# Recurrent layer of a fused block: outputs and norm by tokens in column strips, state products in row strips

## The reference, cut to what matters

```python
proj = h @ w_in                                   # [512, 4 * 1024]
q_x, f_x, i_x, g_x = jnp.split(proj, [HK, 2 * HK, 2 * HK + HV], axis=-1)
f = lb + (1.0 - lb) * sigmoid(f_x);  q = heads(silu(q_x));  k = heads(1.0 - f);  v = heads(i_x)
b = cumsum(log(f)) within each chunk of 32;  b_ref = b[16], b_last = b[31] of the chunk
q_rel, k_rel = q * exp(b - b_ref), k * exp(b_ref - b)
a = where(causal, q_rel @ k_rel.T, 0.0)           # 32 x 32 in each chunk
o_intra = a @ v
q_dec, k_dec, chunk_decay = q * exp(b), k * exp(b_last - b), exp(b_last)
def step(state, xs):                              # 16 chunks in order, state 128 x 128
    o_inter = qd @ state
    state = dec[..., None] * state + kd.T @ vc
o = rms_norm(o_intra + o_inter, o_norm) * silu(g_x)   # norm over the 128 channels of the head
return o @ w_o
```

## Time and profile before

| | us |
|---|---|
| median of three runs | 2893.7 |
| lowest, highest | 2890.9, 2904.2 |
| profiled execution, span from its first to its last instruction | 2894.7 |
| PE busy | 2755.6 (95%) |
| DVE busy | 1621.2 (56%) |
| ACT busy | 1137.4 (39%) |
| POOL busy | 122.3 (4%) |

### The profile page before, as it was taken

The page is one execution under the profiler, slowest core; times in us unless marked ns, Lnnn a source line. Parts: engine busy times, 40 slices in busy tenths (PEclk is TensorE's granted clock), DMA queues, the critical chain, the costliest instruction groups (busy, mean ns, idle before and its releaser), DMA issues.

```text
span 2894.7 us, 39160 instructions
## 1 busy us (share of the span) xinstructions
PE 2755.6 (95%) x14119; PEld 2223.8 (77%) x14119; DVE 1621.2 (56%) x3030; ACT 1137.4 (39%) x1894; POOL 122.3 (4%) x106
## 2 busy tenths in 40 slices
PE   7999999999999999998998998999999989999998
PEld 5567888888888788887685886667877777788887
DVE  6335726456665662645656337765577765564461
ACT  4434322225553422223438324852355543322221
POOL 0000000000000000000130001000011110000000
PEclk9999999999999999998999989999999999999999
DMA  4112333312211233331220221013222222333232
GB/s 139 43 59 73 109 95 94 102 52 67 67 63 37 80 114 97 95 97 58 64 81 1 73 74 30 1 44 95 80 66 73 66 66 73 124 102 98 92 101 65
DMA packets 59684, 217.83 MB, mean 75 GB/s; under 512 B 6432, under 2 KB 6560, under 8 KB 59424
## 3 DMA queue, kind: packets, MB, share of 16 engines
q1 hardware_dynamic: 57920, 209.76, 23.5%
q0 software_dynamic: 1632, 6.29, 0.6%
HBM read 211.83 MB, written 4.19 MB: 75 GB/s over the span
## 4 chain that ended last, share of the span: by engine, by line
PE 81%; DVE 10%; ACT 3%; issue 3%; DVEq 2%; ACTq 0%; DMA 0%; POOL 0%; SPq 0%
PE ps L371 23%; PE ps L373 22%; PE ps L372 22%; DVE work L2095 1%; PE ps L512 1%; DVE big L3254 1%; DVEq L3312 1%; DVE work L2114 1%; DVE ring_lo L311 1%; PE ps L763 1%; PE ps L1564 1%; PE ps L1640 1%; PE ps L2020 1%; PE ps L2256 1%; ACT ring_hi L304 1%
## 5 line engine op out<-in xcount | busy, mean ns | idle before, releaser
L371 PE MATMUL ps<-a_hi,ring_hi 128*128 128x512 f32 (+1 forms) x1976 | 781.7, 396 | 42.7 <-DVE ring_lo L311 24.0
L373 PE MATMUL ps<-a_hi,ring_lo 128*128 128x512 f32 (+1 forms) x1976 | 766.4, 388 | 0.0
L372 PE MATMUL ps<-a_lo,ring_hi 128*128 128x512 f32 (+1 forms) x1912 | 739.7, 387 | 0.0
L311 DVE TENSOR_TENSOR ring_lo<-ring,ring_hi 128x1024 fp32r<-128x1024 f32 x357 | 436.7, 1225 | 519.5 <-ACT ring_hi L304 489.6
L304 ACT ACTIVATE ring_hi<-ring 128x1024 fp32r<-128x1024 f32 x377 | 396.7, 1055 | 505.8 <-PE ps L373 503.6
L371 PEld LDWEIGHTS ps<-a_hi,ring_hi 128*128 128x128 f32 x1976 | 376.5, 191 | 125.0 <-DVE ring_lo L311 18.1
L373 PEld LDWEIGHTS ps<-a_hi,ring_lo 128*128 128x128 f32 x1976 | 375.9, 190 | 76.7
L372 PEld LDWEIGHTS ps<-a_lo,ring_hi 128*128 128x128 f32 x1912 | 364.2, 190 | 70.1 <-issue 1.2
L372 PE MATMUL ps<-hid_lo,ring_hi 128*128 128x512 f32 (+1 forms) x992 | 381.0, 384 | 0.0
L371 PE MATMUL ps<-hid_hi,ring_hi 128*128 128x512 f32 (+1 forms) x928 | 354.5, 382 | 0.0
L373 PE MATMUL ps<-hid_hi,ring_lo 128*128 128x512 f32 (+1 forms) x928 | 354.2, 382 | 0.0
(11 more groups left out here) (419 smaller groups left out, 3369.3 us busy)
## 6 DMA issues: line engine op xcount, KB each, us to landing
ring<-weights SPq DMA_DIRECT2D x392, 512.0 KB, 3.6
h<-x SPq DMA_DIRECT2D x1, 2048.0 KB, 9.4
residual<-h POOLq DMA_DIRECT2D x4, 512.0 KB, 3.5
h<-residual POOLq DMA_DIRECT2D x1, 2048.0 KB, 10.9
out<-h POOLq DMA_DIRECT2D x1, 2048.0 KB, 7.9
tab<-tables SPq DMA_DIRECT2D x1, 1648.0 KB, 15.5
big<-positions SPq DMA_DIRECT2D x1, 256.0 KB, 3.4
col<-columns SPq DMA_DIRECT2D x1, 164.5 KB, 4.1
```

Of the source, the lines that this page charges most:

```text
L311: dve.tensor_tensor(lo, M.ring[:, b % RING, :], hi.bitcast(F32), ALU.subtract).then_inc(M.sem("blocks_split"), 1)
L371: pe.matmul(out, w_hi, hi, start=start, stop=False)
L372: pe.matmul(out, w_hi, lo, start=False, stop=False)
L373: return pe.matmul(out, w_lo, hi, start=False, stop=stop)
```

## The change

The state products take the turned keys as they are (`kt`, one copy of 128 partitions), and use 32 rows of the array each: keys and values of chunk r lie on partitions 32r to 32r + 31, so the matmul uses row strip r. The four strips write to four different banks (4, 5, 6, 7). All 15 that are needed come in one go before slice 5 of projection 2, behind waits on `hg_v`, `hg_keys_kept`, `hg_pairs_masked` and `hg_y`. DVE's chain waits for them once.

The outputs have tokens on the partitions: masked pairs stationary and values moving, then 32 tokens of q_dec stationary and a state moving, which uses column strip r of the array and writes partitions 32r to 32r + 31 of bank 7. The first chunk, whose state is zero, is left out. The sum over channels is then along the free axis: ACT takes four squares with an accumulator, the root at once, and after DVE's reciprocal four copies scaled by the inverse root of each token (`ot`). PE turns them back with four transposes (`turn_out`) behind projection 1 of the next head, and DVE applies gate and gain with one L1807. `total` and `spread`, L1810, the zeros of `kz` and the wait for `hg_y` before the pairs are gone.

```diff
+PAIR_BANK, KEY_BANK, OUT_T_BANK, OUT_BANK = 4, 5, 6, 7
+STATE_BANK = (PAIR_BANK, KEY_BANK, OUT_T_BANK, OUT_BANK)
...
-        self.kz = M.m[:, 0:4, :]
+        self.kt, self.ot = M.m[:, 0, :], M.m[:, 1, :]
...
-    dve.memset(R.kz, 0.0)
...
-            if k == (4 if j else 6) and between:
+            if k == 5 and between:
...
-    def states(tt, bank):
-        for r in range(4):
-            mm = pe.matmul(M.bank(bank)[:, r * P:(r + 1) * P], R.kz[:, r, tt * P:(tt + 1) * P],
-                           R.v[:, tt * P:(tt + 1) * P], start=True, stop=True)
+    def states():
+        for t in range(QT):
+            for r in range(4):
+                if 4 * t + r < N_CH - 1:
+                    rows, s = slice(CH * r, CH * r + CH), slice(t * P, (t + 1) * P)
+                    mm = pe.matmul(M.bank(STATE_BANK[r])[:, s], R.kt[rows, s], R.v[rows, s], start=True, stop=True)
         mm.then_inc(M.sem("hg_chunk_states"), 1)
-    def total(i):
-        pe.wait_ge(M.sem("hg_squared"), i + 1)
-        norm_total_pe(pe, M, M.bank(7), M.sq[:, 0, :]).then_inc(M.sem("hg_total"), 1)
-    def spread(i):
-        pe.wait_ge(M.sem("hg_inverse"), i + 1)
-        norm_spread_pe(pe, M, M.bank(7), lambda c: M.inv[:, c:c + 1].broadcast_to([P, P]))\
-            .then_inc(M.sem("hg_spread"), 1)
+    def turn_out(i):
+        pe.wait_ge(M.sem("hg_scaled"), i + 1)
+        for t in range(QT):
+            s = slice(t * P, (t + 1) * P)
+            mm = pe.transpose(M.bank(OUT_T_BANK)[:, s], R.ot[:, s], M.t("ident", P))
+        mm.then_inc(M.sem("hg_out_turned"), 1)
+    def out(i):
+        pe.wait_ge(M.sem("hg_pairs_masked"), i + 1)
+        pe.wait_ge(M.sem("hg_chained"), i * 4 + 3)
+        for t in range(QT):
+            s = slice(t * P, (t + 1) * P)
+            pe.matmul(M.bank(OUT_BANK)[:, s], R.masked[:, s], R.v[:, s], start=(t == 0), stop=False,
+                      skip_group_check=True)
+        for c in range(1, N_CH):
+            t, r = c // 4, c % 4
+            if c == N_CH - 4:
+                pe.wait_ge(M.sem("hg_chained"), i * 4 + 4)
+            mm = pe.matmul(M.bank(OUT_BANK, slice(CH * r, CH * r + CH))[:, t * P:(t + 1) * P],
+                           R.q_dec[:, c * CH:(c + 1) * CH], R.state[:, c, :], start=False, stop=(c >= N_CH - 4),
+                           skip_group_check=True)
+        mm.then_inc(M.sem("hg_out"), 1)
     part = lambda u, ks: part_of_tile_pe(pe, M, "hgrn_o", u, R.y_hi, R.y_lo, ks)
     def head(i, nxt, prev):
         if nxt:
-            project(0, i, 1, (lambda: total(i - 1)) if prev else None)
-            project(1, i, 1, (lambda: spread(i - 1)) if prev else None)
+            project(0, i, 1)
+            project(1, i, 1)
+            if prev:
+                turn_out(i - 1)
         elif prev:
             pe.wait_ge(M.sem("hg_banks_free"), 8)
             pe.wait_ge(M.sem("hg_y_split"), 6)
             part(0, range(0, 6))
-            total(i - 1)
-            spread(i - 1)
             part(1, range(0, 4))
+            turn_out(i - 1)
...
-        if prev:
-            pe.wait_ge(M.sem("hg_y"), i)
...
-            mm = pe.matmul(M.bank(4)[:, s], R.k_rel[:, s], R.q_rel[:, s], start=True, stop=True)
+            mm = pe.matmul(M.bank(PAIR_BANK)[:, s], R.k_rel[:, s], R.q_rel[:, s], start=True, stop=True)
...
-            mm = pe.transpose(M.bank(5)[:, s], R.k_dec[:, s], M.t("ident", P))
+            mm = pe.transpose(M.bank(KEY_BANK)[:, s], R.k_dec[:, s], M.t("ident", P))
...
+        def added_states():
+            pe.wait_ge(M.sem("hg_v"), i + 1)
+            pe.wait_ge(M.sem("hg_keys_kept"), i + 1)
+            pe.wait_ge(M.sem("hg_pairs_masked"), i + 1)
+            if prev:
+                pe.wait_ge(M.sem("hg_y"), i)
+            states()
         if nxt:
-            project(2, i, 1)
-        pe.wait_ge(M.sem("hg_v"), i + 1)
-        if not nxt:
+            project(2, i, 1, added_states)
+            project(3, i, 1)
+            turn_values(i, 1)
+        else:
             part(1, range(4, 6))
             part(2, range(0, 3))
-        pe.wait_ge(M.sem("hg_keys_kept"), i + 1)
-        states(0, 6)
-        states(1, 5)
-        if not nxt:
+            added_states()
             part(2, range(3, 6))
-        def last_states():
-            pe.wait_ge(M.sem("hg_chained"), i * 4 + 1)
-            states(2, 6)
-            pe.wait_ge(M.sem("hg_chained"), i * 4 + 2)
-            states(3, 5)
-        if nxt:
-            project(3, i, 1, last_states)
-            turn_values(i, 1)
-        else:
-            last_states()
             pe.wait_ge(M.sem("hg_y_split"), 7)
             for u in range(3):
                 part(u, range(6, 7))
-        pe.wait_ge(M.sem("hg_chained"), i * 4 + 4)
-        pe.wait_ge(M.sem("hg_pairs_masked"), i + 1)
-        for t in range(QT):
-            s = slice(t * P, (t + 1) * P)
-            pe.matmul(M.bank(4)[:, s], R.v[:, s], R.masked[:, s], start=(t == 0), stop=False,
-                      skip_group_check=True)
-            for r in range(4):
-                c = 4 * t + r
-                w = slice(c * CH, (c + 1) * CH)
-                mm = pe.matmul(M.bank(4)[:, w], R.state[:, c, :], R.q_dec[:, w], start=False, stop=(c == N_CH - 1),
-                               skip_group_check=True)
-        mm.then_inc(M.sem("hg_out"), 1)
+        out(i)
...
-    total(7)
-    spread(7)
     pe.wait_ge(M.sem("hg_gate_free"), 8)
     part(3, range(0, 7))
+    turn_out(7)
...
-        for r in range(4):
-            rows = slice(32 * r, 32 * r + 32)
-            act.activation(R.kz[rows, r, :], M.bank(5, rows), ACT.Copy)
-        act.drain().then_inc(M.sem("hg_keys_kept"), 1)
+        act.activation(R.kt, M.bank(KEY_BANK), ACT.Copy).then_inc(M.sem("hg_keys_kept"), 1)
...
         act.wait_ge(M.sem("hg_out"), i + 1)
-        act.activation(M.sq[:, 0, :], M.bank(4), ACT.Square).then_inc(M.sem("hg_squared"), 1)
+        for t in range(QT):
+            s = slice(t * P, (t + 1) * P)
+            act.activation(M.sq[:, 0, s], M.bank(OUT_BANK)[:, s], ACT.Square, accum_out=M.root[:, QT + t:QT + t + 1])
+        act.drain()
+        act.activation(M.root[:, 0:QT], M.root[:, QT:2 * QT], ACT.Sqrt, bias=M.eps, scale=1.0 / P)\
+           .then_inc(M.sem("hg_root"), 1)
         if nxt:
             values(i, 1)
-        act.wait_ge(M.sem("hg_total"), i + 1)
-        act.activation(M.root[:, 0:QT], M.bank(7)[:, 0:QT], ACT.Sqrt, bias=M.eps, scale=1.0 / P)\
-           .then_inc(M.sem("hg_root"), 1)
+        act.wait_ge(M.sem("hg_inverse"), i + 1)
+        for t in range(QT):
+            s = slice(t * P, (t + 1) * P)
+            act.activation(R.ot[:, s], M.bank(OUT_BANK)[:, s], ACT.Copy, scale=M.inv[:, t:t + 1])
+        act.drain().then_inc(M.sem("hg_scaled"), 1)
...
-                            M.bank(4).rearrange("p (a b) -> p a b", a=QT))
+                            M.bank(PAIR_BANK).rearrange("p (a b) -> p a b", a=QT))
...
-            dve.wait_ge(M.sem("hg_chunk_states"), i * 4 + (t + 1))
+            if t == 0:
+                dve.wait_ge(M.sem("hg_chunk_states"), i + 1)
...
+                added = M.bank(STATE_BANK[r])[:, t * P:(t + 1) * P]
                 dve.scalar_tensor_tensor(out=R.state[:, c + 1, :], in0=R.state[:, c, :],
                                          scalar=R.e_b[:, c * CH + 31:c * CH + 32],
-                                         in1=M.bank(6 - t % 2)[:, r * P:(r + 1) * P], op0=ALU.mult, op1=ALU.add)
+                                         in1=added, op0=ALU.mult, op1=ALU.add)
...
-        dve.wait_ge(M.sem("hg_spread"), i + 1)
-        dve.scalar_tensor_tensor(out=R.norm, in0=R.gate, scalar=M.c("o_norm"), in1=M.bank(7),
-                                 op0=ALU.mult, op1=ALU.mult)
-        dve.drain()
-        dve.tensor_tensor(R.norm, R.norm, M.bank(4), ALU.mult).then_inc(M.sem("hg_y"), 1)
+        dve.wait_ge(M.sem("hg_out_turned"), i + 1)
+        dve.scalar_tensor_tensor(out=R.norm, in0=R.gate, scalar=M.c("o_norm"), in1=M.bank(OUT_T_BANK),
+                                 op0=ALU.mult, op1=ALU.mult).then_inc(M.sem("hg_y"), 1)
```

## The result

The changed kernel takes 2855.07 us (median of four runs, 2849.57 to 2860.3) against 2898.95 for the kernel before beside it (four runs, 2890.9 to 2905.38): a ratio of 0.9847, with a 95% interval of 0.982 to 0.9874. Forecast were 2854, within 2844 to 2870. The profiled execution has a span of 2847.7, 47.0 less than the one of before.

The account below looks back on a forecast made before the run. PE was taken to bound the kernel; its 6.1 us saved per head became 5.0 through DVE's loop over bank 0. Head 0 2.3, six heads 30 and last section 7.5 make 40 off 2894.7: 2855, so 2854, range 2844 to 2870.

Parts of the forecast that it names:

- rival 1: Four strips run only two at a time: 1.0 a head, 2862, 15%; no overlap at all: 2885, 5%.
- Wait (a): PE's projection waits until DVE's L1751 has read bank 0: 0.8 us a head.
- S: The point in a head where the state products end.
- Wait (b): PE's output transposes need ACT's hg_scaled: hidden, with 1.2 us to spare.
- P: The point where a head's value transposes start.
- Wait (c): PE waits for DVE's hg_pairs_masked before the state products: 0.4 us, at no cost to the head.
- The last section: From L1686 of head 7 to the first L371 after the partial tiles: net 7.5 us saved, after 2 lost to clock.
- T: The point where the new transposes of the outputs end.
- Rival 2: ACT's chain to hg_scaled ends last, 1.6 us late in each head: 2864; chance 7%.
- Rival 3: PE idles of 0.8 and 0.4 in each head bring the half clock, 1.7 us a head: 2867; chance 7%.
- Rival 4: No wait shows, since DVE gets through its steps sooner: 27.7 us a head, 2847; chance 8%.
- Rival 5: Strips don't overlap and load anew at each change, 0.31 us per matmul, slower than before: 2908; chance 3%.

Follow-up runs that it names:

- e9: Changed kernel with three DVE moves: block 2's L311 and k behind the product reading bank 0, q_dec behind the reciprocal; 2845.1 us, ratio to before 0.9816.
- e1: Changed kernel with the strip matmuls of states and outputs issued strip after strip instead of alternating; 2868.63 us.
- e2: Changed kernel with the state products alone put back on the full array with zero-padded keys; 2874.31 us, ratio to before 0.9914.
- e5: Changed kernel with DVE's L311 for block 2 moved behind the product that reads bank 0; 2851.12 us.
- e4: Changed kernel with three extra, unused 128x1024 copies on ACT ahead of the squares; 2866.05 us.
- e3: Changed kernel with one extra, unused 128x1024 copy on ACT ahead of the squares; 2858.52 us.
- e10: Kernel of e9 with the last section's output transposes ahead of the last two partial tiles of part(3); 2844.49 us, ratio to before 0.9815.
- e11: The changed kernel unedited, run again beside e9 and e10 on the same chip; 2858.25 us, ratio to before 0.9865.

## Why the prediction was right, by its own steps

**The strips cost what perfect overlap costs.** The value taken was 0.89 for a group (rival 1 would have had twice that). The states cost 1.10 from their start to the next projection matmul, and 0.09 on entering, as e9 shows, where nothing is waited for ahead of them: 1.19, 1.25 forecast. The outputs cost 2.07, 2.2 forecast. Four records start together:

```profile
795.20:795.26 0.06, 0.03 (x4) 1.00 0.00 0
```

The row of two records within 0.10 did carry to four strips. Under strict starts, the Trainium skill's rule in "TensorE: Matmul & The Clock Gate", The mechanism, the second pass of a matmul would stand ahead of the next one's first, if the rule is read for single passes, as the prediction read it; the page names whole matmuls. Read for passes, this trace doesn't agree for matmuls in different strips, with four records within 0.06. Read for whole matmuls, e1's doesn't: a strip's first starts ahead of the last one of the strip before, which stands earlier in the stream. e1 also gives the condition that the prediction lacked: each matmul's neighbour in the stream has to be of another strip.

**Wait (a), bank 0.** Forecast 0.8, measured 0.71, with the same releaser. The two sides of it, from S: 10.9 for DVE (11.1 forecast; S of the head before is 0.1 ahead of its L371 at 767.54), and 10.2 for PE. That this loop sets the head is shown by e2, where 2.42 more in it gave 2.45, and by e5.

**Wait (b), ACT.** Forecast hidden with 1.2 to spare; e4 gives 1.4, and e3 over 1.1. The scaled copies ended at P + 12.7 (787.9), forecast 13.2 with the semaphore, and PE came at P + 14.2, forecast 14.4. The four squares took 1.2 in place of 1.4, since an accumulator read lies beside the next square.

**Wait (c), the mask.** Forecast 0.4, measured 0.47, released by the mask's drain.

**A head.** 28.75 forecast, 28.77 to 28.86 measured; PE's own work 27.7 forecast, 27.60 where nothing is waited for (e9). Six heads: 30 forecast, 29.9. Head 0: 2.3 forecast, 2.33.

**The last section.** 7.5 forecast, 9.17 measured, and here one term was mis-sized. The steps held: PE idles 2.49 before the transposes and 2.15 behind part(3) (3 and 2.4 forecast), and T is P + 13.7 as forecast (875.24, with P = 861.57). The mis-sized one is "the longer idles will have as much, at worse places: 2 lost" (and 2.9 + 6.8 - 2 is 7.7, not 7.5). From T to the first slice behind the split lie 22.29 (to 897.53) where 21.8 was worked out at full clock, and from there to the end of the section 4.51 where it was 4.32 before: 0.7 lost. Half clock had 10.2 of the section before and has 6.8 now. The second stretch of it costs next to nothing, since the end of the section was held by DVE's rounding of a block in the kernel before:

```profile
943.57 0.47 PE L371 MATMUL ps<-hid_lo,ring_hi 128*128 128x512 f32 x1 [1.43 <-DVE ring_lo L311]
```

In the changed kernel PE, at half clock, comes too late to wait there; in e10, at full clock, the wait is back. For the stage that makes 41.4, against 40.

**The total.** The forecast of 2854 against a median of 2855.07 is closer than its parts deserve, and that is luck. The sum itself gave a profiled span of 2855, and the span is 2847.7. The span fell by 47.0, the medians by 43.9 in this comparison and by 38.05 in e11's, while the stage gave 41.4. Both kernels' runs spread over some 10 us, e.g. 2849.57, 2850.36, 2859.77 and 2860.3 for the changed one, with mean clocks of 0.983, 0.982, 0.978 and 0.979: some 0.4% of the span. Where in the common code each run gets or loses its clock was not traced, so this is a correlation and stays open. The windows of the heads repeat within 0.1 and are the better measure.

**What fell.** Rival 1: four records start together and the state group costs 1.2, not the 2.0 of two strips at a time; strips in series, as in e1, take the head to 30.6 and the time to 2868.63, between the rival's two prices. Rival 2: ACT releases the transposes only in head 7. Rival 3: the clock stood at 1.00 in the heads with idles of 0.71 and 0.47, and even of up to 1.82 in e4. Rival 4 is e9, after three moves on DVE. Rival 5 needs 0.25 for each matmul; the worst order gave 0.17.

## What to carry to other kernels

Fifteen small fp32 products that fill only a quarter of the array's rows cost a third of the full-array ones when four strips alternate (1.17 against 3.59 in e2), and 0.7 of their time when strip follows strip (2.56): put neighbours in the stream into different strips. Price a shortening of the busiest engine by the loops that it closes with the others (here 6.2 of work became 5.0 of time), and then look on the other engine for instructions that stand ahead of a release without need: three of them, moved, gave back the other 1.2. After each move, look for the second releaser, as e5 got 0.43 of a wait of 0.71.

## What the runs showed of the hardware that was not expected

A group of 15 matmuls in four strips took 2.56 in the order strip after strip (row strips) and 2.24 (column strips, outputs), against 1.17 and 1.07 alternating. In strip after strip, the first matmul of a strip starts 0.01 behind the last but one of the strip before it and ahead of the last, each time, in both groups. So fp32 matmuls of different strips can start out of the order of the stream, but here by one place only; what sets this reach stays open.

The clock after an idle isn't set by the idle's length alone. In the kernel before, PE idled 1.14 ahead of L461 at 905.25 and its clock was at 0.50, the lower of its two levels, right behind it. In the changed kernel, PE idled 2.49 and was at 0.50 right behind it; in e9 it idled 3.41 at the same place in the program, and the clock stayed at 1.00:

```profile
870.00:874.00 4.00, 3.42 (x23) 3.15 (x24) 2.23 (x4) 1.11 (x3) 0.00 (x0) 1.00 0.45 135
874.00:878.00 4.00, 4.00 (x43) 3.13 (x42) 1.79 (x5) 0.00 (x0) 0.00 (x0) 1.00 0.00 0
```

In head 0, e9 stood at 0.50 from 665 to 670, where the changed kernel had 0.88, behind the same wait of about 3 for bank 0; that head was 29.82 and 28.85. So the best scheme loses 1 us there, and a gain of a few us in total can hide behind such phases.

Four squares of 128x128 with an accumulator followed each other every 0.25 us on ACT, and so did the four scaled copies of the same size without one (the last starts 0.75 behind the first), so the accumulator's read (0.19 to 0.22 each) costs nothing that can be seen here.
